# Modulation panels of the opening stretch multiplied in two portions, with projection chunks between them

## The chip, the cores and the metric

The kernel runs on one core of a Trainium2 chip. Its time is the device time of one execution in microseconds (us), lower is better. The kernel before took 673.79 us, the median of three executions (672.49 to 673.83).

## The reference

One inference step of a hybrid diffusion backbone with one layer: 128 context tokens and 512 latent tokens of 1024 features, all in float32. The parts that the edited stretch computes are the first lines:

```python
mod = silu(cond) @ w_mod + b_mod      # (2, 6*1024): one row per condition (latent, context)
shift1, scale1, gate1, shift2, scale2, gate2 = split(mod, 6)
h = rmsnorm(x, g_pre1) * (1 + scale1) + shift1
z = h @ w_in                          # columns [q | k | v | B | C | u], 512 each
```

After them come differential attention in four heads, a gated short convolution in 512 channels, the output projection, and a hierarchical mixture of 16 experts. They are not touched.

## The kernel before

There is one program for each engine, written out in order, and semaphores between them. An engine executes its program strictly in that order, so the order of the TensorE program around the change is the order written in the source.

**Modulation panels.** Before any column of h exists, shift1 and scale1 are needed, 2048 columns of `w_mod`. They are computed in four panels. Panel n brings 256 columns of shift and the same 256 of scale, that is what the feature chunks 2n and 2n+1 of h need (a chunk is 128 of the 1024 features). `mod_early(n)` multiplies the conditions (32 columns wide, two of them used) by the panel: 8 matmuls, k = 0 to 7, over the 8 chunks of the contraction. Matmul k writes the strip of 32 partitions that begins at 32 * (k % 4) in bank 4 + n % 2 of PSUM, so each strip collects two of them. The panel's weights come in four loads r = 0 to 3, load r with k = 2r and 2r+1, in a ring of eight slots; each pair of matmuls signals `mod_q`.

**From a panel to h.** VectorE adds the bias (`mod_rows_out`, L1207), TensorE turns the rows to columns and sums strips by four transposes (`mod_cols`, L1727) with a reduction on VectorE (L1213 in `mod_columns`), which then writes the shift B1 and factor A1 of two chunks and signals `a1_ready`. For each chunk k, TensorE transposes four latent blocks of x (`h_transposes(k)`, L1763; the context block in `ctx_transposes`, L1756, four chunks at a time), ScalarE applies A1 and B1 to the 512 latent columns (L797), VectorE to the 128 context columns (`h_ctx`, L1229), ScalarE rounds all 640 (L801), and VectorE forms the rest that the rounding left (`h_lo`, L1234, signals `hT_ctx`). Products use three passes over such rounded and rest parts. The weights of the projection are split in the same way, ScalarE (L782) and VectorE (`split_lo`, L1200).

**Projection chunks.** `z_first(k)` (L1772) multiplies chunk k for three token blocks at once: banks 3, 6 and 7, three passes each, 9 matmuls. It waits for `hT_ctx` of its chunk, and for the weights' split at even k. The eight chunks are set between the panels by hand. After chunk 7 the row products `z_rows` (L1839) follow, 24 matmuls a block, with modulation groups and transposes between them.

**Queues.** SyncE issues all weight loads in order: panel n's eight DMAs (L462), then load n of the projection's first weights (L489). From panel 2 on a load waits until the slot's old load is multiplied. GpSimd waits for the fourth `a1_ready` ahead of the loads of the rope tables (L621 to L623).

`lam_mm` are two products with one column each for the scalar lambda. They write columns of banks 6 and 3, which chunk 0 writes later; VectorE copies them out first (`lam_cp`).

Of the kernel before, what the change touches and what calls it, by code (L numbers as in the profile page):

```python
# [29 lines left out]
P = 128  # L30
D = 1024
KC = D // P
# [4 lines left out]
H, DV, DQ = 4, 128, 64  # L37
# [9 lines left out]
MOD_EARLY = 4  # L47
# [16 lines left out]
def build(nc, a):  # L64
# [16 lines left out]
    with ctx:  # L81
        def sb(name, shape, dt=F32):
            return ctx.enter_context(nc.sbuf_tensor(name, shape, dt))
# [20 lines left out]
        ones = sb("ones", [P, P])  # L104
# [7 lines left out]
        ps = ctx.enter_context(nc.psum_tensor("ps", [P, 8, N], F32))  # L112
# [14 lines left out]
        def col(i, n=1):  # L127
            return small[:, i:i + n]
# [7 lines left out]
        lamp = col(99)  # L136
        nlam = col(100)
        epsc = col(101)
        lamw = col(102, 4)
# [81 lines left out]
        def early_slot(j):  # L221
            return qkv[:, (j % 8) * D:(j % 8 + 1) * D]
# [945 lines left out]
        def _(dve):  # L1168
            n_chain = [0]

            def link(ins):
                n_chain[0] += 1
                ins.then_inc(S["dve_chain"], 1)
                dve.wait_ge(S["dve_chain"], n_chain[0])
# [10 lines left out]
            link(nc.vector.tensor_copy(small[:, 16:39], ps[:, 6, 0:23]))  # L1185
            link(ts(subg, subg, 1.0 - LAM_INIT, None, ALU.mult))
            tt(lamp, lamq[:, 0:1], lamq[:, 1:2], ALU.mult).then_inc(S["lam_prod"], 1)

            dve.wait_ge(S["rms1"], 1)
            link(nc.vector.reciprocal(rstd, rt))  # L1190
# [3 lines left out]
            def split_lo(item):  # L1194
                kind, c, r = item
                n = place[kind, c]
                m = 6 * P if kind == "conv" else QUARTER
                slot, rslot = (4 * n + r) % SPLIT, at_ring[item] % RAW
                dve.wait_ge(S["hi"], 4 * n + r + 1)
                tt(spl[:, slot, 1, 0:m], raw[:, rslot, 0:m], spl[:, slot, 0, 0:m].bitcast(F32), ALU.subtract).then_inc(S["lo"], 1)  # L1200

            def mod_rows_out(n):
                dve.wait_ge(S["mod_q"], 4 * (n + 1))
                if n >= 2:
                    dve.wait_ge(S["col_mm"], n - 1)
                both = lambda ap, m: ap.rearrange("p (s n) -> p s n", s=2)[:, :, m:m + CHUNK]
                tt(both(rows_early[n % 2], 0), both(ps[:, 4 + n % 2, :], 0), both(bias_early, n * CHUNK), ALU.add).then_inc(S["mod_ev"], 1)  # L1207

            def mod_columns(n):
                dve.wait_ge(S["col_mm"], n + 1)  # L1210
                ks = slice(2 * n, 2 * n + 2)
                parts = ps[:, 4 + n % 2, :].rearrange("p (j g m) -> p j m g", j=4, g=4)[:, :, 0:2, :]
                link(nc.vector.reduce_sum(cols_early.rearrange("p (j c) -> p j c", c=2), parts, axis=AX))  # L1213
                sh = cols_early[:, 0:4].rearrange("p (k c) -> p c k", c=2)
                sc = cols_early[:, 4:8].rearrange("p (k c) -> p c k", c=2)
                nc.vector.tensor_copy(B1[:, :, ks], sh)
                stt(A1[:, 0, ks], sc[:, 0, :], 1.0, gpre1[:, ks], ALU.add, ALU.mult)
                link(stt(A1[:, 1, ks], sc[:, 1, :], 1.0, gpre1[:, ks], ALU.add, ALU.mult))
                ts(col(183), epsc, 1.0, None, ALU.mult).then_inc(S["a1_ready"], 1)

            def hf_rows(k):
                return work[:, TOK * (k % 2):TOK * (k % 2 + 1)]

            def h_ctx(k):
                dve.wait_ge(S["h_trc"], k // 4 + 1)
                if k >= 2:
                    dve.wait_ge(S["hT_ctx"], k - 1)
                o = (k % 4) * P
                ts(hf_rows(k)[:, L_LAT:TOK], ps[:, 2, o:o + P], A1[:, 1, k:k + 1], B1[:, 1, k:k + 1],  # L1229
                   ALU.mult, ALU.add).then_inc(S["hf_ctx"], 1)  # L1230

            def h_lo(k):
                dve.wait_ge(S["hT_lat"], k + 1)
                tt(hS[:, 1, k, :], hf_rows(k), hS[:, 0, k, :].bitcast(F32), ALU.subtract).then_inc(S["hT_ctx"], 1)  # L1234
            dve.wait_ge(S["bmod_in"], 16)
            mod_rows_out(0)
            split_lo(("in", 0, 0))
            mod_columns(0)
            h_ctx(0)
            h_ctx(1)  # L1240
            h_lo(0)
            dve.wait_ge(S["lam_mm"], 1)
            nc.vector.tensor_copy(lamw[:, 0:1], ps[:, 6, 0:1]).then_inc(S["lam_cp"], 1)
            nc.vector.tensor_copy(lamw[:, 1:2], ps[:, 3, 0:1]).then_inc(S["lam_cp"], 1)
            for n in range(1, MOD_EARLY):
                mod_rows_out(n)
                h_lo(2 * n - 1)
                split_lo(("in", 0, n))
                mod_columns(n)
                h_ctx(2 * n)  # L1250
                h_lo(2 * n)
                h_ctx(2 * n + 1)
            h_lo(KC - 1)
            split_lo(SPLITS[2][0])

            def rope_rows(g):
# [446 lines left out]
        def _(pe):  # L1703
            mm = nc.tensor.matmul
# [3 lines left out]
                    pe.wait_ge(S["lo"], 4 * n + k // 2 + 1)  # L1708
            PASSES = ((0, 0), (0, 1), (1, 0))

            def mod_early(n):
                if n >= 2:
                    pe.wait_ge(S["a1_ready"], n - 1)
                for k in range(KC):
                    j = 4 * n + k // 2
                    if k % 2 == 0:
                        pe.wait_ge(early[j % 8], 32 * (j // 8 + 1))
                    g = 32 * (k % 4)
                    ins = mm(ps[g:g + 32, 4 + n % 2, :], condz[:, k, :], early_slot(j)[:, (k % 2) * N:(k % 2 + 1) * N],
                             start=(k < 4), stop=(k >= 4))  # L1720
                    if k % 2:
                        ins.then_inc(S["mod_q"], 1)

            def mod_cols(n):
                pe.wait_ge(S["mod_ev"], n + 1)
                for j in range(4):
                    ins = nc.tensor.transpose(ps[:, 4 + n % 2, j * P:(j + 1) * P], rows_early[n % 2][:, j * P:(j + 1) * P], ident[:, :])  # L1727
                ins.then_inc(S["col_mm"], 1)
# [20 lines left out]
            def ctx_transposes(f):  # L1749
                if f == 0:  # L1750
                    pe.wait_ge(S["xn_ready"], TB)
                else:
                    pe.wait_ge(S["hf_ctx"], 4)
                for j in range(4):
                    k = 4 * f + j
                    ins = nc.tensor.transpose(ps[:, 2, j * P:(j + 1) * P], x[:, CTX, k * P:(k + 1) * P], ident[:, :])  # L1756
                ins.then_inc(S["h_trc"], 1)

            def h_transposes(k):
                if k >= 2:  # L1760
                    pe.wait_ge(S["hf_lat"], k - 1)
                for b in range(4):
                    ins = nc.tensor.transpose(ps[:, k % 2, b * P:(b + 1) * P], x[:, b, k * P:(k + 1) * P], ident[:, :])  # L1763
                ins.then_inc(S["h_tr"], 1)

            def z_first(k):
                n = place["in", 0]
                pe.wait_ge(S["hT_ctx"], k + 1)
                part_ready(n, k)
                for g, bank in enumerate((3, 6, 7)):  # L1770
                    for s, m in PASSES:
                        ins = mm(ps[:, bank, :], hS[:, s, k, g * P:(g + 1) * P], weight(n, k, m),  # L1772
                                 start=(k == 0 and s + m == 0), stop=(k == KC - 1 and s == 1))
                    if k == KC - 1:
                        ins.then_inc(S["z_mm"], 1)
# [4 lines left out]
            pe.wait_ge(S["stage_in"], 16 * 7)  # L1780
            nc.tensor.transpose(ps[:, 6, 0:23], vrow, ident[0:23, 0:23]).then_inc(S["rows_tr"], 1)
            pe.wait_ge(S["cols_ready"], 2)
            mod_early(0)
            ctx_transposes(0)
            h_transposes(0)
            h_transposes(1)
            mod_cols(0)
            pe.wait_ge(S["lam_prod"], 1)
            mm(ps[:, 6, 0:1], ones[0:DQ, :], lamp[0:DQ, :], start=True, stop=True)
            mm(ps[:, 3, 0:1], ones[DQ:P, :], lamp[DQ:P, :], start=True, stop=True).then_inc(S["lam_mm"], 1)  # L1790
            mod_early(1)
            pe.wait_ge(S["lam_cp"], 2)
            z_first(0)
            mod_cols(1)
            h_transposes(2)
            h_transposes(3)
            z_first(1)
            mod_early(2)
            z_first(2)
            mod_cols(2)  # L1800
            ctx_transposes(1)
            h_transposes(4)
            h_transposes(5)
            z_first(3)
            mod_early(3)
            z_first(4)
            mod_cols(3)
            h_transposes(6)
            h_transposes(7)
            z_first(5)  # L1810
            z_first(6)
            z_first(7)

# [450 lines left out]
```

## Time and profile before

| | us |
|---|---|
| median of three executions | 673.79 |
| the profiled execution, its own time | 672.04 |
| its span, first to last instruction | 670.1 |
| TensorE (PE) busy | 639.0, 95% |
| VectorE (DVE) busy | 510.9, 76% |
| ScalarE (ACT) busy | 416.0, 62% |
| GpSimd (POOL) busy | 110.8, 17% |
| matmuls and weight loads | 3570 each |

The mean granted clock of TensorE is 0.995 of full speed. "PE" is a matmul, "PEld" the load of its stationary operand beside it; queues that issue DMAs have a q behind the engine's name (SPq is SyncE's). The ends of matmuls are modelled, so that one printed duration holds a fixed latency that the next matmul overlaps; what a group occupies is read from its start to the start of the next group. The 8 float32 matmuls of a panel are recorded as 16 instructions.

### The profile page before, as it was taken

The numbers are of one execution on the slowest core, as the hardware profiler recorded it, in microseconds if no ns is written. First come the engines' busy times: TensorE is split into PE (matmuls) and PEld (weight loads), VectorE is DVE, ScalarE is ACT, GpSimd is POOL, SyncE is SP. The second block draws the span as 40 slices with busy tenths as digits, with TensorE's granted clock in tenths as the row PEclk, the third lists the DMA queues.
The fourth block names the chain that finished last, engine by engine and source line by source line (L and its number), as shares of the span: only waits on it lengthen the run. The fifth ranks groups of instructions, "written<-read, shape, count | busy, mean of one in ns | idle before, by whom it ended". The sixth has DMA issues, their size and how long they took to land.

```text
span 670.1 us, 11052 instructions
## 1 busy us (share of the span) xinstructions
PE 639.0 (95%) x3570; PEld 524.3 (78%) x3570; DVE 510.9 (76%) x755; ACT 416.0 (62%) x640; POOL 110.8 (17%) x172
## 2 busy tenths in 40 slices
PE   2999999999999999999998899999999999999993
PEld 0577767889999998888786688888888888888872
DVE  2666576767676767775876988898989999899986
ACT  5552122344747486763445687888888888888873
POOL 2041000165000000000011650000000000290151
PEclk9999999999999999999999999999999999999997
DMA  9965768549212134495488799999999999999886
GB/s 332 386 244 184 264 242 254 156 148 336 64 34 59 62 101 151 147 324 189 159 313 320 251 336 419 419 420 420 420 420 420 420 420 419 416 403 376 320 308 157
DMA packets 77148, 188.16 MB, mean 281 GB/s; under 512 B 7824, under 2 KB 29381, under 8 KB 77109
## 3 DMA queue, kind: packets, MB, share of 16 engines
q1 hardware_dynamic: 65408, 153.11, 61.9%
q0 software_dynamic: 7392, 22.47, 9.8%
q10 hardware_dynamic: 4310, 12.10, 4.5%
q8 instruction: 22, 0.36, 0.2%
q14 instruction: 16, 0.12, 0.0%
HBM read 166.12 MB, written 21.53 MB: 280 GB/s over the span
## 4 chain that ended last, share of the span: by engine, by line
PE 77%; DVE 6%; DMA 6%; POOL 3%; ACT 2%; SPq 2%; issue 2%; POOLq 0%; ACTq 0%; DVEq 0%
PE ps L2128 20%; PE ps L2148 11%; PE ps L1839 10%; PE ps L1863 7%; PE ps L1895 6%; PE ps L1867 5%; PE ps L1916 3%; PE ps L1939 2%; PE ps L1772 2%; PE ps L2104 2%; SPq L462 2%; DMA catT_mem<-token_rows,rows_now 2%; PE ps L1930 2%; PE ps L1737 1%; DMA expert_rows<-catT_mem 1%
## 5 line engine op out<-in xcount | busy, mean ns | idle before, releaser
L2128 PE MATMUL ps<-split_ring,split_rows 128*128 128x512 f32 x720 | 168.3, 392 | 1.7 <-DVE split_rows L1568 1.0
L1485 DVE TENSOR_TENSOR split_ring<-qkv_mem,split_ring 128x1024 fp32r<-128x1024 f32 x124 | 144.0, 1221 | 23.4 <-ACT split_ring L970 23.2
L2128 PEld LDWEIGHTS ps<-split_ring,split_rows 128*128 128x128 f32 x720 | 133.9, 188 | 30.3 <-DVE split_ring L1485 1.6
L970 ACT CAST split_ring<-qkv_mem 128x1024 fp32r<-128x1024 f32 x124 | 121.1, 1053 | 9.3 <-ACT catT_mem L1076 9.3
L1863 PE MATMUL ps<-split_rows,split_ring 128*128 128x384 f32 x288 | 87.1, 349 | 0.2 <-ACT work L905 0.2
L2148 PE MATMUL ps<-split_ring,split_rows 128*128 128x512 f32 x360 | 86.3, 395 | 0.0
L2148 PEld LDWEIGHTS ps<-split_ring,split_rows 128*128 128x128 f32 x360 | 66.6, 188 | 13.6
L1867 PE MATMUL ps<-split_rows,split_ring 128*128 128x256 f32 x288 | 77.0, 280 | 0.0
L1485 DVE TENSOR_TENSOR split_ring<-raw_ring,split_ring 128x1024 fp32r<-128x1024 f32 x64 | 74.3, 1221 | 0.0
L1839 PE MATMUL ps<-split_ring,split_rows 128*128 128x512 f32 x288 | 68.0, 393 | 0.0
L970 ACT CAST split_ring<-raw_ring 128x1024 fp32r<-128x1024 f32 x64 | 62.4, 1046 | 0.9 <-DMA raw_ring<-in_w_exp_up 0.9
L1839 PEld LDWEIGHTS ps<-split_ring,split_rows 128*128 128x128 f32 x288 | 53.4, 188 | 10.8
L782 ACT CAST split_ring<-raw_ring 128x1024 fp32r<-128x1024 f32 (+1 forms) x36 | 34.2, 959 | 41.2 <-DMA raw_ring<-in_w_in 41.2
L1895 PE MATMUL ps<-split_ring,split_rows 128*128 128x512 f32 x240 | 58.4, 396 | 0.7 <-DVE split_ring L1200 0.7
L1200 DVE TENSOR_TENSOR split_ring<-raw_ring,split_ring 128x1024 fp32r<-128x1024 f32 (+1 forms) x36 | 39.5, 1102 | 23.3 <-ACT split_ring L782 22.9
L1863 PEld LDWEIGHTS ps<-split_rows,split_ring 128*128 128x128 f32 x288 | 53.5, 189 | 1.4 <-issue 1.3
L1867 PEld LDWEIGHTS ps<-split_rows,split_ring 128*128 128x128 f32 x288 | 53.4, 188 | 0.0
L1895 PEld LDWEIGHTS ps<-split_ring,split_rows 128*128 128x128 f32 x240 | 44.0, 188 | 10.3 <-DVE split_ring L1200 1.0
L1341 DVE TENSOR_REDUCE small<-ps 128x1 f32<-128x640 f32 (+1 forms) x40 | 26.8, 712 | 12.9 <-PE ps L1916 12.7
L1064 ACT CAST split_rows<-ps 128x512 fp32r<-128x512 f32 x30 | 16.1, 590 | 32.3 <-PE ps L2104 32.3
L626 POOL DMA_DIRECT2D x_rows<-in_b_mod x10 | 5.1, 513 | 181.5 <-DMA out_lat<-x_rows 181.5
L674 POOL TENSOR_TENSOR rows_now<-token_lists 128x1 uint32<-128x1 uint32 x13 | 5.2, 396 | 169.3 <-PE ps L2104 169.2
(361 smaller groups left out, 919.1 us busy)
## 6 DMA issues: line engine op xcount, KB each, us to landing
qkv_mem<-in_w_exp_gate SPq DMA_DIRECT2D x64, 512.0 KB, 8.3
qkv_mem<-in_w_exp_up SPq DMA_DIRECT2D x60, 512.0 KB, 7.0
raw_ring<-in_w_exp_down SPq DMA_DIRECT2D x60, 512.0 KB, 8.0
raw_ring<-in_w_mod SPq DMA_DIRECT2D x26, 512.0 KB, 4.5
qkv_mem<-in_w_mod SPq DMA_DIRECT2D x32, 256.0 KB, 7.0
expert_rows<-catT_mem ACTq DMA_DIRECT2D x14, 512.0 KB, 6.6
expert_rows<-work POOLq DMA_DIRECT2D x26, 256.0 KB, 5.9
raw_ring<-in_w_in SPq DMA_DIRECT2D x12, 512.0 KB, 6.4
```

The source lines that it names most:

```text
L782: nc.scalar.copy(spl[:, (4 * n + r) % SPLIT, 0, 0:m], raw[:, q % RAW, 0:m]).then_inc(S["hi"], 1)
L970: nc.scalar.copy(moe_split(tile, j, r, 0), moe_raw(tile, j, r)).then_inc(S["hi"], 1)
L1200: tt(spl[:, slot, 1, 0:m], raw[:, rslot, 0:m], spl[:, slot, 0, 0:m].bitcast(F32), ALU.subtract).then_inc(S["lo"], 1)
L1341: nc.vector.reduce_max(nm[:, u % 2, c:c + 1], psf[:, SC[c]:SC[c] + nk], axis=AX, negate=True).then_inc(S["neg_max"], 1)
L1485: tt(moe_split(tile, j, r, 1), moe_raw(tile, j, r), moe_split(tile, j, r, 0).bitcast(F32), ALU.subtract).then_inc(S["lo"], 1)
L1839: ins = mm(ps[:, g % 2, :], hS[:, s, k, b * P:(b + 1) * P], weight(n, k, m), start=(k == 0 and s + m == 0), stop=(k == KC - 1 and s == 1))
L1863: return mm(ps[:, CONV_BANK, 0:LOW], conv_weight(n, k, s, part), hS[:, m, k, 0:LOW], start=(k == 0 and s + m == 0), stop=(k == KC - 1 and ...
L1867: return mm(ps[:, CONV_BANK + 1, 0:HIGH], conv_weight(n, k, s, part), hS[:, m, k, LOW:TOK], start=(k == 0 and s + m == 0), stop=(k == KC - ...
L1895: ins = mm(ps[:, banks + j, :], cS[:, s, b, kk, :], weight(place["o", j], kk, m), start=(kk == 0 and s + m == 0), stop=(kk == KC - 1 and s ...
L1916: ins = mm(psf[:, SC[c] + o:SC[c] + o + m], q[rows, :], key[rows, :], start=(s + w == 0), stop=(s == 1))
L2128: ins = mm(ps[:, j, :], rows[:, s, k * P:(k + 1) * P], moe_split(tile, j, k // 2, m)[:, (k % 2) * N:(k % 2 + 1) * N], start=(k == 0 and s ...
L2148: ins = mm(ps[:, 5 + half, :], aS[:, s, k, :], spl[:, moe_split_slot(turn, j, k), m, half * N:(half + 1) * N], start=(k == 0 and s + m == ...
```

## The change

TensorE multiplies loads 0 to 2 of panels 1, 2 and 3, then a projection chunk, and then load 3 of the panel. Two of the three banks of the next odd chunk come ahead of the panel's column transposes, its third bank behind them. The column transposes of panel 0 go ahead of the transposes of chunk 1. Chunk 5 goes ahead of the transposes of chunks 6 and 7, chunk 3 ahead of those of 4 and 5. The lambda products go to the front of the program. VectorE's program becomes one loop over panels, with `split_lo` behind `mod_columns` and `h_ctx`, and the lambda copies ahead of the norm's reciprocal.

```diff
@@ VectorE, start
             tt(lamp, lamq[:, 0:1], lamq[:, 1:2], ALU.mult).then_inc(S["lam_prod"], 1)
+            dve.wait_ge(S["lam_mm"], 1)
+            nc.vector.tensor_copy(lamw[:, 0:1], ps[:, 6, 0:1]).then_inc(S["lam_cp"], 1)
+            nc.vector.tensor_copy(lamw[:, 1:2], ps[:, 3, 0:1]).then_inc(S["lam_cp"], 1)
@@ VectorE, panels
-            mod_rows_out(0)
-            split_lo(("in", 0, 0))
-            mod_columns(0)
-            h_ctx(0)
-            h_ctx(1)
-            h_lo(0)
-            dve.wait_ge(S["lam_mm"], 1)
-            nc.vector.tensor_copy(lamw[:, 0:1], ps[:, 6, 0:1]).then_inc(S["lam_cp"], 1)
-            nc.vector.tensor_copy(lamw[:, 1:2], ps[:, 3, 0:1]).then_inc(S["lam_cp"], 1)
-            for n in range(1, MOD_EARLY):
+            for n in range(MOD_EARLY):
                 mod_rows_out(n)
-                h_lo(2 * n - 1)
-                split_lo(("in", 0, n))
                 mod_columns(n)
                 h_ctx(2 * n)
+                split_lo(("in", 0, n))
                 h_lo(2 * n)
                 h_ctx(2 * n + 1)
-            h_lo(KC - 1)
+                h_lo(2 * n + 1)
             split_lo(SPLITS[2][0])
@@ TensorE, helpers
-            def mod_early(n):
+            def mod_early(n, rs=range(4)):
...
-                for k in range(KC):
+                for k in (2 * r + i for r in rs for i in range(2)):
...
-            def z_first(k):
+            def z_first(k, gs=range(3)):
...
-                for g, bank in enumerate((3, 6, 7)):
+                for g in gs:
+                    bank = (3, 6, 7)[g]
@@ TensorE, order
             pe.wait_ge(S["cols_ready"], 2)
+            pe.wait_ge(S["lam_prod"], 1)
+            mm(ps[:, 6, 0:1], ones[0:DQ, :], lamp[0:DQ, :], start=True, stop=True)
+            mm(ps[:, 3, 0:1], ones[DQ:P, :], lamp[DQ:P, :], start=True, stop=True).then_inc(S["lam_mm"], 1)
             mod_early(0)
             ctx_transposes(0)
             h_transposes(0)
+            mod_cols(0)
             h_transposes(1)
-            mod_cols(0)
-            pe.wait_ge(S["lam_prod"], 1)
-            mm(ps[:, 6, 0:1], ones[0:DQ, :], lamp[0:DQ, :], start=True, stop=True)
-            mm(ps[:, 3, 0:1], ones[DQ:P, :], lamp[DQ:P, :], start=True, stop=True).then_inc(S["lam_mm"], 1)
-            mod_early(1)
+            mod_early(1, range(3))
             pe.wait_ge(S["lam_cp"], 2)
             z_first(0)
+            mod_early(1, (3,))
+            h_transposes(2)
+            z_first(1, (0, 1))
             mod_cols(1)
-            h_transposes(2)
+            z_first(1, (2,))
             h_transposes(3)
-            z_first(1)
-            mod_early(2)
+            mod_early(2, range(3))
             z_first(2)
+            mod_early(2, (3,))
+            z_first(3, (0, 1))
             mod_cols(2)
+            z_first(3, (2,))
             ctx_transposes(1)
             h_transposes(4)
             h_transposes(5)
-            z_first(3)
-            mod_early(3)
+            mod_early(3, range(3))
             z_first(4)
+            mod_early(3, (3,))
+            z_first(5, (0, 1))
             mod_cols(3)
+            z_first(5, (2,))
             h_transposes(6)
             h_transposes(7)
-            z_first(5)
             z_first(6)
             z_first(7)
```

## Rows read from the trace of the kernel before

**Rows 1.** The page: busy time of the engines, and the chain that ended last.
```profile
PE 639.0 (95%) x3570; PEld 524.3 (78%) x3570; DVE 510.9 (76%) x755; ACT 416.0 (62%) x640; POOL 110.8 (17%) x172
PE 77%; DVE 6%; DMA 6%; POOL 3%; ACT 2%; SPq 2%; issue 2%; POOLq 0%; ACTq 0%; DVEq 0%
```
**Rows 2.** Waits of TensorE: line, waited for, us in total, times, longest.
```profile
PE ps L1719 <- DMA qkv_mem<-in_w_mod: 3.5, 3, 2.9
...
PE ps L2104 <- DMA catT_mem<-token_rows,token_lists: 2.2, 1, 2.2
```
**Rows 3.** Busy time in stretches: stretch, its us, engines, PEclk, DMA share, GB/s.
```profile
360.00:375.00 15.00, 11.79 (x56) 9.17 (x55) 11.89 (x30) 7.72 (x10) 2.73 (x4) 1.00 0.74 262
...
400.00:600.00 200.00, 199.56 (x947) 166.15 (x946) 181.28 (x180) 162.31 (x191) 32.92 (x44) 1.00 1.03 419
```
**Rows 4.** Timeline of TensorE, 12 to 56 us: start, us, instructions, idle before.
```profile
12.36 5.84 PE L1719 MATMUL ps<-qkv_mem,cond_columns 128*32 128x512 f32 x16 [2.90 <-DMA qkv_mem<-in_w_mod]
...
20.34 1.07 PE L1719 MATMUL ps<-qkv_mem,cond_columns 128*32 128x512 f32 x8
21.74 1.05 PE L1719 MATMUL ps<-qkv_mem,cond_columns 128*32 128x512 f32 x4 [0.34 <-DMA qkv_mem<-in_w_mod]
23.09 1.05 PE L1719 MATMUL ps<-qkv_mem,cond_columns 128*32 128x512 f32 x4 [0.30 <-DMA qkv_mem<-in_w_mod]
24.07 2.34 PE L1772 MATMUL ps<-split_ring,split_rows 128*128 128x512 f32 x9
...
29.75 1.92 PE L1719 MATMUL ps<-qkv_mem,cond_columns 128*32 128x512 f32 x16
...
33.79 0.60 PE L1727 MATMUL ps<-ident,catT_mem 128*128 128x128 f32 x4
...
34.66 1.04 PE L1763 MATMUL ps<-ident,x_rows 128*128 128x128 f32 x8
...
41.76 0.60 PE L1727 MATMUL ps<-ident,catT_mem 128*128 128x128 f32 x4
...
42.99 2.33 PE L1772 MATMUL ps<-split_ring,split_rows 128*128 128x512 f32 x9
45.60 4.44 PE L1772 MATMUL ps<-split_ring,split_rows 128*128 128x512 f32 x18 [0.28 <-DVE split_rows L1234]
49.87 5.60 PE L1839 MATMUL ps<-split_ring,split_rows 128*128 128x512 f32 x24
55.40 1.06 PE L1737 MATMUL ps<-raw_ring,cond_columns 128*32 128x512 f32 x8
```
**Rows 5.** Timeline of TensorE, 29.7 to 30.5 us: the first half of panel 2.
```profile
29.75 1.06 PE L1719 MATMUL ps<-qkv_mem,cond_columns 128*32 128x512 f32 x8
```
**Rows 6.** Timeline of VectorE, 18 to 46 us.
```profile
18.31 0.69 DVE L1207 TENSOR_TENSOR catT_mem<-ps,catT_mem 128x512 f32<-128x512 f32 x1 [1.06 <-PE ps L1719]
...
41.05 1.22 DVE L1200 TENSOR_TENSOR split_ring<-raw_ring,split_ring 128x1024 fp32r<-128x1024 f32 x1
42.40 0.19 DVE L1213 TENSOR_REDUCE small<-ps 128x8 f32<-128x32 f32 x1
...
43.05 0.41 DVE L1229 TENSOR_SCALAR work<-ps,small 128x128 f32<-128x128 f32 x1
44.72 0.82 DVE L1234 TENSOR_TENSOR split_rows<-work,split_rows 128x640 fp32r<-128x640 f32 x1 [1.26 <-ACT split_rows L801]
```
**Rows 7.** Timeline of ScalarE, 35 to 45 us.
```profile
35.34 0.78 ACT L797 ACTIVATE work<-ps,small 128x512 f32<-128x512 f32 x1 [3.16 <-PE ps L1763]
...
43.15 0.78 ACT L797 ACTIVATE work<-ps,small 128x512 f32<-128x512 f32 x1 [3.33 <-DVE small L1219]
43.96 0.73 ACT L801 CAST split_rows<-work 128x640 fp32r<-128x640 f32 x1
```
**Rows 8.** Timelines of SyncE and GpSimd, 24 to 46 us: DMA issues.
```profile
24.67 5.84 SPq L462 DMA_DIRECT2D qkv_mem<-in_w_mod  x8
...
42.30 7.00 SPq L489 DMA_DIRECT2D raw_ring<-in_w_in  x2
...
43.42 1.76 POOL L621 DMA_DIRECT2D catT_mem<-rope  x2 [38.51 <-DVE small L1219]
```

## The prediction

> **What bounds the kernel now.** I read the page first, then the waits of TensorE, then its busy time in stretches, and last the timelines of the first 55 us, because the whole diff lies there.
>
> The page shows a TensorE that is busy 95% of the span and holds 77% of the chain that ended last [rows 1]. Its waits name what is left: the start of the kernel, and single waits of 1 to 2 us around 365 to 385 us [rows 2]. In the expert stage it is busy 199.6 of 200 us, with the DMA engines full beside it [rows 3]. So a microsecond that TensorE loses early has nowhere to be made up, and only idle time that it has today can be won.
>
> How much is that in the edited stretch? In the timeline of TensorE [rows 4] look for the bracket with an idle time. Between the first panel (12.36) and 49.87, where the row products of L1839 begin, there are three: 0.34 and 0.30 ahead of panel 1's third and fourth loads, and 0.28 ahead of chunk 6 at 45.60. Everything else is back to back. The edit's prize is thus about 1 us; what matters is what it costs.
>
> **Prices.** From the starts in [rows 4], since the printed ends overlap:
> - A projection chunk is 9 matmuls (3 banks, 3 passes). 24 of the same shape go from 49.87 to 55.40, 0.230 each: 2.07 a chunk, 1.38 for two banks, 0.69 for one.
> - Eight transposes go from 33.79 to 34.66: 0.435 for four.
> - A whole modulation panel, with its entry and exit: 33.79 to 41.76 is 7.97. In it are 16 transposes (1.74), two chunks (4.14) and one panel, which is left with 2.09.
> - A panel in portions. A panel is 8 matmuls, recorded as 16 instructions, that write four strips of 32 partitions (k mod 4). Load r brings k = 2r and 2r+1, so loads 0 and 1 fill four strips, load 2 strips 0 and 1, load 3 strips 2 and 3. The first 8 instructions of an undisturbed panel take 1.06 [rows 5]. The 4 of a single load take 1.05, both at 21.74 and at 23.09, and loads 0 and 1 together took 1.07 at 20.34 [rows 4]. So four instructions on two strips last as long as eight on four: strips run side by side, and half of them save nothing. Hence a portion of three loads costs what all four cost (2.09), and load 3 by itself costs a panel less two of its four time slots: 2.09 less (1.92 less 1.05) = 1.22. Its bounds: 0.44, a quarter of 1.92 less its tail, if the slot were shared after all, and 1.37, which is 1.05 with an entry and exit of 0.16 each. I take 1.22.
>
> **The change, part by part.**
>
> 1. The two lambda products and their two copies go ahead of panel 0. TensorE waits for the first load until 12.36 and VectorE for rms1 long after; behind the products loads 2 and 3 of panel 1 are waited for anyway. Worth 0 (bounds: 0.3 won, 0.3 lost).
>
> 2. Panel 0's column transposes go ahead of chunk 1's transposes. They need mod_rows_out(0), VectorE at 18.31 plus 0.69 = 19.00 [rows 6], when eight transposes have just ended, so they start at about 19.05. From here a chain returns that I use four times. Read it after panel 3: column transposes at 41.76 [rows 4]; VectorE reduces at 42.40 (+0.64) and has A1 and B1 written by 43.1; ScalarE's ACTIVATE starts at 43.15 (0.75 after the reduce), its CAST at 43.96 [rows 7]; h_lo at 44.72 [rows 6]; TensorE's chunk at 45.60. From reduce to chunk 3.20, from ACTIVATE to chunk 2.45. In the new VectorE order h_ctx (0.41) and split_lo (1.22) stand between reduce and h_lo; they end 2.2 after the reduce, h_lo could start at 2.32 at the earliest, so they are hidden behind ScalarE. For chunk 0: 19.05 + 0.64 + 3.20 = 22.9. TensorE has by then done loads 0 to 2 of panel 1 (21.74 + 1.05 = 22.8). Chunk 0 starts at 22.9 instead of 24.07: 1.17 won.
>
> 3. Then the order is walked with the prices; a restart after a wait costs 0.1 as in 45.60 (the 18 there take 4.27, not 4.14). Chunk 0 ends 25.07, load 3 26.29, transposes 2 26.73, two banks of chunk 1 28.11, columns 1 28.55, third bank 29.24, transposes 3 29.68, three loads of panel 2 31.77. Chunk 2 may start at 28.11 + 0.64 + 3.20 = 31.95: wait 0.2. Then it ends 34.12, load 3 35.34, two banks 36.72, columns 2 37.16, third bank 37.85, context transposes 38.29, transposes 4 and 5 39.16, three loads of panel 3 41.25. Chunk 4 hangs on ScalarE's ACTIVATE, which starts about 0.25 after transposes 4 (34.66 + 0.44 to 35.34 before [rows 4, 7]): 38.72 + 0.25 + 2.45 = 41.42: wait 0.2. It ends 43.59, load 3 44.81, two banks 46.19, columns 3 46.63, third bank 47.32, transposes 6 and 7 48.19.
>
> 4. Now chunk 6. Before, chunk 5's nine matmuls lay between transposes 7 and chunk 6 and covered the chain but for 0.28. In the new order chunk 5 is used up ahead of the transposes. ACTIVATE 6 waits for A1 (46.19 + 0.64 + 0.75 = 47.58) and for transposes 6 (47.76 + 0.25 = 48.01); chunk 6 starts at 48.01 + 2.45 = 50.46. TensorE has nothing from 48.19 on: a wait of 2.3 in place of the 0.28. Chunk 7's rows are ready 1.9 after that, in time.
>
> So chunk 6 starts at 50.46 against 45.60: **4.9 us later**. The same by causes: start -1.2; load 3 by itself, three times 1.22, +3.65; two waits of 0.2, each with a restart, +0.6; the longer wait for chunk 6, +1.8 (its restart was there before, and so were 0.45: the recorded 0.28 is counted from a modelled end, chunk 5 had been issued by 42.99 + 0.08 + 2.07 = 45.15); together +4.9. I take 4.8.
>
> What else moves: the DMA issues. SyncE's loads of panel 3 begin at 24.67 and end at 30.5 [rows 8]; the last waits for load 3 of panel 1, now at 26.3 instead of 24.1, while its issue comes near 29: nothing. The ring's next load waits for the fourth split, 42.3 before (41.05 + 1.22, [rows 6, 8]), about 49 now; it feeds the second part of the projection, two blocks of row products (11 us) behind chunk 7. GpSimd's rope loads wait for the last A1, 43.4 before [rows 8], about 47.7 now, less late than TensorE. All later waits shift with TensorE. The cost passes through whole; I see no slack that would hide more than 0.5 of it.
>
> The clock: the granted clock is 1.00, its 2.4 GHz level, from 360 to 375 us [rows 3], and in that stretch TensorE stood idle for 2.2 us before L2104 [rows 2]. My new wait is 2.3, so I leave the clock alone. The Trainium skill, TensorE: Matmul & The Clock Gate, section HAM oscillation, warns that waits between bursts of matmuls can drop the clock to half, and that this cost is paid anew at each burst. By that rule the 18 matmuls of chunks 6 and 7 would take 8.3 instead of 4.1 and the sum be about 9.
>
> **Against what time.** The profiled execution took 672.04 (span 670.1, 1.9 around it); the three others 672.49, 673.79 and 673.83. The middle of the four is 673.1. With 4.8 the likely median is 677.9.
>
> **Rivals.**
> - *The single load is cheap* (0.44 to 0.5 instead of 1.22, three times): 2.2 less, +2.6, 675.7. For it: [rows 4] show single loads only right after a DMA wait. Against: 20.34 and 29.75 are not after one and have the same slots. 11%.
> - *The clock falls* in the wait for chunk 6: +9, 682. Against: the idle time of 2.2 at clock 1.00. 4%.
> - *Not slower*: the expert stage is set by its weight stream, not by TensorE (DMA share 1.03 in [rows 3]), and the stream starts at a time that the early stretch doesn't move. Place: 400 to 600 us; price: the whole 4.8 back; it decides if TensorE there has 4.8 us of waiting for weights hidden in its modelled ends. Then 673. Against: it issues without a wait in that stretch, and SyncE's first expert loads stand behind waits for TensorE's results. 4%.
> - *The new waits don't appear*, since the split gives ScalarE and VectorE their rows earlier: then the single loads and the earlier start remain, +2.4, 675.5. For it: chunks 0 to 5 do get their rows earlier. Against: the chain to chunk 6 begins at the column transposes of panel 3, and just 0.69 + 0.87 of work stands behind them. 6%.
>
> **How the numbers follow.** The forecast has 75%. This kernel tells no change from one of about 0.2% (1.3 us). Slower by more: the forecast and three rivals, 0.95 with a little for their neighbours, less what I may have misread as a whole: 0.93. Within: 0.04. Faster: 0.03. The range runs from the cheap loads, 675.7 less 0.7 for a low set of executions, to +6 on an execution of 673.8 with a bit of the bounds of load 3: 675.0 to 680.6.
>
> **What would show it.** Right: load 3 as groups of four instructions of 1.05 beside chunks; L1772 starting near 22.9; a wait of about 2.3 on h_lo (L1234 before) ahead of the last 18 matmuls; the first x24 of the row products near 54.7. Wrong: that start under 53, or a wait for chunk 6 under 1.5, or the tail of the kernel not shifted by what the early stretch lost.

## The result and the profile after

The changed kernel takes 677.83 us in the median of eight executions (675.88 to 679.54); the kernel before, with eight of its own, 673.66 (672.00 to 676.18). The ratio is 1.0067, with an interval from 1.0047 to 1.0087: slower, by 4.5 us (3.2 to 5.9) by the ratio and by 4.2 between the medians. Forecast were 677.9 and +4.8. A second set of ten, taken beside the experiments, gave 677.55 and 1.0060 (1.0033 to 1.0086). The profiled execution took 677.10 with a span of 675.1, against 672.04 and 670.1.

The timeline of TensorE after, to be read against [rows 4] (L1712 is the panel, L1720 the column transposes, L1749 and L1756 the transposes of x, L1766 the chunks; start, us, instructions, idle before):

```profile
20.00 1.45 PE L1712 MATMUL ps<-qkv_mem,cond_columns 128*32 128x512 f32 x8
21.72 1.05 PE L1712 MATMUL ps<-qkv_mem,cond_columns 128*32 128x512 f32 x4 [0.27 <-DMA qkv_mem<-in_w_mod]
22.92 2.33 PE L1766 MATMUL ps<-split_ring,split_rows 128*128 128x512 f32 x9
25.17 1.05 PE L1712 MATMUL ps<-qkv_mem,cond_columns 128*32 128x512 f32 x4
...
29.70 1.91 PE L1712 MATMUL ps<-qkv_mem,cond_columns 128*32 128x512 f32 x12
31.88 2.33 PE L1766 MATMUL ps<-split_ring,split_rows 128*128 128x512 f32 x9 [0.27 <-DVE split_rows L1237]
34.14 1.05 PE L1712 MATMUL ps<-qkv_mem,cond_columns 128*32 128x512 f32 x4
35.12 1.66 PE L1766 MATMUL ps<-split_ring,split_rows 128*128 128x512 f32 x6
36.62 0.60 PE L1720 MATMUL ps<-ident,catT_mem 128*128 128x128 f32 x4
...
41.32 2.31 PE L1766 MATMUL ps<-split_ring,split_rows 128*128 128x512 f32 x9 [0.26 <-DVE split_rows L1237]
...
46.03 0.60 PE L1720 MATMUL ps<-ident,catT_mem 128*128 128x128 f32 x4
46.38 0.94 PE L1766 MATMUL ps<-split_ring,split_rows 128*128 128x512 f32 x3
47.16 1.04 PE L1756 MATMUL ps<-ident,x_rows 128*128 128x128 f32 x8
50.29 4.43 PE L1766 MATMUL ps<-split_ring,split_rows 128*128 128x512 f32 x18 [2.10 <-DVE split_rows L1237]
54.56 5.60 PE L1839 MATMUL ps<-split_ring,split_rows 128*128 128x512 f32 x24
```

Three things are to be seen. Twelve instructions of a panel take 1.91, as sixteen did (1.92, [rows 4]), and the last four take another 1.05. The wait ahead of chunk 6 is 2.10 instead of 0.28. And the row products start at 54.56 instead of 49.87: 4.69 of the span's 5.0 are lost by this point.

The chain that makes chunk 6 wait, on VectorE and on ScalarE (against [rows 6, 7]):

```profile
46.67 0.19 DVE L1216 TENSOR_REDUCE small<-ps 128x8 f32<-128x32 f32 x1 [1.32 <-PE ps L1720]
...
47.73 0.41 DVE L1232 TENSOR_SCALAR work<-ps,small 128x128 f32<-128x128 f32 x1 [0.34 <-issue]
48.06 1.22 DVE L1203 TENSOR_TENSOR split_ring<-raw_ring,split_ring 128x1024 fp32r<-128x1024 f32 x1
49.41 0.83 DVE L1237 TENSOR_TENSOR split_rows<-work,split_rows 128x640 fp32r<-128x640 f32 x1
```
```profile
47.85 0.78 ACT L797 ACTIVATE work<-ps,small 128x512 f32<-128x512 f32 x1 [4.49 <-DVE small L1222]
48.66 0.72 ACT L801 CAST split_rows<-work 128x640 fp32r<-128x640 f32 x1
```

From ScalarE's ACTIVATE to chunk 6 it is 2.44, as before (43.15 to 45.60). The chain has not become longer; TensorE has nothing left to do during it.

Behind the row products the shift stays. The waits of TensorE there, after (against [rows 2]):

```profile
PE ps L2104 <- DMA catT_mem<-token_rows,token_lists: 2.3, 1, 2.3
PE ps L2104 <- DMA catT_mem<-token_rows,rows_now: 1.0, 1, 1.0
```

The same transposes L2104 start at 371.56 instead of 366.80 (+4.76), and at 408.03 instead of 402.72 (+5.31, a gather of token rows came 0.5 later in this execution); the end is 5.0 later.

### The profile page after: what moved, and what is told of

The parts are those of the page before. It is cut to its first block, busy times and chain, and to the rows that moved or that the text cites. A ratio compares the mean times of both kernels' runs of the same rounds, so it can differ in the third digit from the quotient of the medians.

```text
span 675.1 us, 11054 instructions
## 1 busy us (share of the span) xinstructions
PE 644.4 (95%) x3570; PEld 526.8 (78%) x3570; DVE 511.3 (76%) x755; ACT 416.2 (62%) x640; POOL 111.6 (17%) x172
## 4 chain that ended last, share of the span: by engine, by line
PE 76%; DVE 6%; DMA 6%; POOL 3%; ACT 3%; issue 2%; SPq 2%; POOLq 0%; ACTq 0%; DVEq 0%
PE ps L2128 20%; PE ps L2148 11%; PE ps L1839 10%; PE ps L1863 7%; PE ps L1895 6%; PE ps L1867 5%; PE ps L1916 3%; PE ps L1939 2%; PE ps L1766 2%; PE ps L2104 2%; DMA catT_mem<-token_rows,rows_now 2%; PE ps L1930 2%; SPq L462 2%; PE ps L1730 1%; DMA catT_mem<-token_rows,token_lists 1%
```

## The experiments

Where a trace gives the verdict I compare starts on TensorE up to the row products. They repeat within 0.1 once it is allowed for that the landing of panel 1's loads moves by up to 0.8 from execution to execution; the whole times of one kernel scatter by 2.4 to 7.1 us. Each ratio is against executions of the kernel before that were taken beside it.

**Whole panels in the new order.**

```diff
-            mod_early(1, range(3))
+            mod_early(1)
...
             z_first(0)
-            mod_early(1, (3,))
```
(panels 2 and 3 likewise)

> The changed kernel with panels 1 to 3 multiplied whole again; the new order of transposes, chunks and of VectorE stays. My theory (a single load by itself costs a half-filled panel, about 1.2 us, and chunk 6 waits because chunk 5 lies ahead of the transposes): chunk 0 starts at 24.1, the three portions of 1.2 are gone, the wait ahead of chunk 6 stays near 2; chunk 6 starts near 48.0 and the row products (L1839) at 52.2, that is 2.3 later than before and 2.3 earlier than the changed kernel; whole time 2.3 us over before. Rival (single loads are cheap, the order alone is the loss): row products at 54 or later. Rival (the portions are the whole loss): row products at 50 to 50.5.

```profile
22.98 1.05 PE L1712 MATMUL ps<-qkv_mem,cond_columns 128*32 128x512 f32 x4 [0.27 <-DMA qkv_mem<-in_w_mod]
...
31.82 3.73 PE L1766 MATMUL ps<-split_ring,split_rows 128*128 128x512 f32 x15 [0.25 <-DVE split_rows L1237]
...
40.08 3.76 PE L1766 MATMUL ps<-split_ring,split_rows 128*128 128x512 f32 x15 [0.24 <-DVE split_rows L1237]
...
47.94 4.38 PE L1766 MATMUL ps<-split_ring,split_rows 128*128 128x512 f32 x18 [2.10 <-DVE split_rows L1237]
52.16 5.60 PE L1836 MATMUL ps<-split_ring,split_rows 128*128 128x512 f32 x24
```

Chunk 6 at 47.94 and row products at 52.16, to a tenth where my theory had them. So at the row products the new order, VectorE's with it, costs 2.3 (52.16 less 49.87) and the portions 2.4 on top (54.56 less 52.16). Both rivals, each with one cause for everything, fall.

The whole times do not show this division. They are 676.05 us (10 executions), ratio 1.0058 (1.0039 to 1.0076): 3.9 us over before, 2.6 to 5.1, and the 2.3 that I expected lies outside. The profiled execution is the fastest of the ten (673.95) and its span is only 1.9 longer than before. Against the changed kernel's 1.0067 and 1.0060 the ratio is barely lower, though 2.4 us would be 0.0036, and each has an uncertainty of about 0.002. What the other executions lost behind the stretch no trace shows.

**Two and two loads.**

```diff
-            mod_early(1, range(3))
+            mod_early(1, (0, 1))
...
             z_first(0)
-            mod_early(1, (3,))
+            mod_early(1, (2, 3))
```
(panels 2 and 3 likewise)

> The changed kernel with each panel in loads 0 and 1, the chunk, then loads 2 and 3. My theory (four strips run side by side, so a portion of two loads with all four strips costs the same 1.2 as a single load with two strips): the second portions are x8 lasting 1.05 to 1.10 as the x4 did, the first portions shorter by a half-filled slot pair (0.9), which the waits ahead of chunks 2 and 4 take up (0.27 becomes about 1.1); row products at 54.5, no change of the time against the changed kernel. Rival (cost goes by the number of instructions): each second portion 0.5 to 1.0 longer, row products 1.5 or more later, at 56.

```profile
29.71 1.06 PE L1712 MATMUL ps<-qkv_mem,cond_columns 128*32 128x512 f32 x8
31.89 2.36 PE L1766 MATMUL ps<-split_ring,split_rows 128*128 128x512 f32 x9 [1.11 <-DVE split_rows L1237]
34.18 1.06 PE L1712 MATMUL ps<-qkv_mem,cond_columns 128*32 128x512 f32 x8
35.17 1.67 PE L1766 MATMUL ps<-split_ring,split_rows 128*128 128x512 f32 x6
...
50.45 6.01 PE L1766 MATMUL ps<-split_ring,split_rows 128*128 128x512 f32 x18 [2.10 <-DVE split_rows L1237]
56.29 5.61 PE L1839 MATMUL ps<-split_ring,split_rows 128*128 128x512 f32 x24
```

Eight instructions on four strips take 1.06 where four on two took 1.05, and what the first portion saves (1.91 less 1.06) goes into the wait ahead of chunk 2 (1.11 instead of 0.27). Up to chunk 6 this kernel runs as the changed one (50.45 against 50.29). So the number of instructions does not set the cost, the fullest strip does. But the row products start at 56.29, the place that I had given to the rival. The second portions are not longer, though, as the rival needs; the cause is another. TensorE in stretches of this run (stretch, its us, busy, PEclk, DMA share, GB/s):

```profile
50.40:52.00 1.60, 1.55 (x7) 0.97 0.83 223
52.00:55.40 3.40, 3.40 (x10) 0.51 0.83 258
```

The granted clock fell to its lower level, 1.2 GHz, at 51.9 and came back at 55.3. TensorE had then been busy again for 1.4 us behind its wait of 2.10 ahead of chunk 6. Chunks 6 and 7 took 1.6 longer (6.01 against 4.43). The time was 677.48 (6 executions), ratio 1.0075 (1.0051 to 1.0099), not to be told from the changed kernel's.

**Chunk 5 back behind the transposes.**

```diff
             mod_early(3, (3,))
-            z_first(5, (0, 1))
             mod_cols(3)
-            z_first(5, (2,))
             h_transposes(6)
             h_transposes(7)
+            z_first(5)
             z_first(6)
```

> The changed kernel with chunk 5 as a whole behind the transposes of chunks 6 and 7, as before; the portions stay. My theory: panel 3 now ends behind chunk 4, so its column transposes have to wait for VectorE's bias rows (end near 45.35, a wait of about 0.8), then 3.84 to chunk 6, with 3.4 of work over it: chunk 6 at 49.25 after a wait of 0.4 to 0.5, row products at 53.5, 1.0 earlier than the changed kernel. Rival (the place of chunk 5 is the whole cause of the wait ahead of chunk 6): row products at 52.5 or earlier. Rival (chunk 6 hangs on something else, the split of the weights or GpSimd): no change, 54.5.

```profile
43.23 1.05 PE L1712 MATMUL ps<-qkv_mem,cond_columns 128*32 128x512 f32 x4
45.08 0.66 PE L1720 MATMUL ps<-ident,catT_mem 128*128 128x128 f32 x4 [0.79 <-DVE catT_mem L1210]
...
49.16 4.42 PE L1766 MATMUL ps<-split_ring,split_rows 128*128 128x512 f32 x18 [0.46 <-DVE split_rows L1237]
53.41 5.60 PE L1838 MATMUL ps<-split_ring,split_rows 128*128 128x512 f32 x24
```

As expected: the wait ahead of chunk 6 shrinks from 2.10 to 0.46, and a new one of 0.79 opens ahead of the column transposes, because the panel's last load now ends right before them and they need VectorE's bias rows. From load 3 of panel 3 to the row products it is 10.18, against 11.00 in the changed kernel (43.56 to 54.56): 0.8 won, of 1.0 expected. So the place of chunk 5 makes the long wait ahead of chunk 6; about half of the 1.6 taken off it comes back as the other wait, which in the changed kernel two banks of chunk 5 had covered. The 0.46 that is left is VectorE's order, as the next kernels show. The whole time does not show the 0.8: 676.71 (6 executions), ratio 1.0068 (1.0042 to 1.0094), the changed kernel's.

**Only the first panel in portions**, everything from chunk 1 on in the old order. The edit of the TensorE order is shown against the kernel before; the lambda products, panel 0's column transposes and VectorE's program are as in the changed kernel.

```diff
-            mod_early(1)
+            mod_early(1, range(3))
             pe.wait_ge(S["lam_cp"], 2)
             z_first(0)
-            mod_cols(1)
+            mod_early(1, (3,))
             h_transposes(2)
             h_transposes(3)
+            mod_cols(1)
             z_first(1)
```

> The kernel before with the early part of the change alone: lambda products first, column transposes of panel 0 ahead of chunk 1's transposes, panel 1 in portions with chunk 0 between, VectorE's new order; all behind as before. My theory: chunk 0 starts at 22.9, 1.15 earlier, but load 3 behind it costs 1.2, so chunk 2 starts at 31.6 as before and the row products at 49.8 to 49.9; same time as before. Rival (filling the wait for the load wins 1 us): row products at 48.8. Rival (VectorE's new order costs, its split now in the chain): row products at 50.5 or later.

```profile
22.93 2.33 PE L1766 MATMUL ps<-split_ring,split_rows 128*128 128x512 f32 x9 [0.29 <-issue]
25.18 1.05 PE L1712 MATMUL ps<-qkv_mem,cond_columns 128*32 128x512 f32 x4
...
31.55 2.37 PE L1766 MATMUL ps<-split_ring,split_rows 128*128 128x512 f32 x9
...
45.76 4.45 PE L1766 MATMUL ps<-split_ring,split_rows 128*128 128x512 f32 x18 [0.47 <-DVE split_rows L1237]
50.05 5.61 PE L1834 MATMUL ps<-split_ring,split_rows 128*128 128x512 f32 x24
```

672.69 against 672.79, ratio 1.0001 (0.9986 to 1.0016). Chunk 0 starts 1.14 earlier and chunk 2 as before (31.55 against 31.60). Even where the multiplication of a load was waited for, starting the chunk first gives nothing: the load's 1.2 comes after it. Chunk 6 is 0.16 late, which I hadn't counted.

**VectorE's new order without portions**: the kernel above with panel 1 whole and its column transposes ahead of the transposes of chunks 2 and 3. The lambda products and panel 0's column transposes stay at their new places.

```diff
-            mod_early(1, range(3))
+            mod_early(1)
             pe.wait_ge(S["lam_cp"], 2)
             z_first(0)
-            mod_early(1, (3,))
+            mod_cols(1)
             h_transposes(2)
             h_transposes(3)
-            mod_cols(1)
```

> The kernel before with the lambda products first, the column transposes of panel 0 ahead of chunk 1's transposes, and VectorE's new order; panels whole, chunks in the old order. My theory: chunk 0 starts at 24.0 as before (load 3 lands at 23.05), and the one cost is VectorE's: with the panel in portions alone chunk 6 had started 0.15 late, because the split of the weights now stands between h_ctx and h_lo of chunk 6 and h_ctx starts 0.4 late; row products at 50.0, against 49.87. Time the same as before within 0.2%. Rival (that 0.15 came from the portions): row products at 49.8.

```profile
22.30 1.05 PE L1712 MATMUL ps<-qkv_mem,cond_columns 128*32 128x512 f32 x4 [0.28 <-DMA qkv_mem<-in_w_mod]
...
45.00 4.45 PE L1766 MATMUL ps<-split_ring,split_rows 128*128 128x512 f32 x18 [0.47 <-DVE split_rows L1237]
49.29 5.61 PE L1833 MATMUL ps<-split_ring,split_rows 128*128 128x512 f32 x24
```

Load 3 landed 0.79 earlier here (22.30 against 23.09); from it to the row products it is 26.99 against 26.78 before, so 0.2 is lost behind load 3. The wait ahead of chunk 6 is 0.47, as with the portions: the 0.16 did not come from them. VectorE's timeline has the cause: h_ctx starts at 42.66, 0.34 after the engine was free, and the split of the weights behind it holds h_lo until 44.12, while ScalarE's CAST had ended at 43.90. 673.66, ratio 1.0000 (0.9976 to 1.0025).

**Filling the gaps.** Where TensorE waits for loads 2 and 3 of panel 1, transposes fit that have to be done anyway; and the bank split of the change, used on chunk 4, covers VectorE's step ahead of panel 3's column transposes, with chunk 5 left behind them. Panels 2 and 3 stay whole; VectorE's new order stays. The edit is shown against the kernel just above.

```diff
             h_transposes(1)
-            mod_early(1)
+            mod_early(1, (0, 1))
             pe.wait_ge(S["lam_cp"], 2)
+            h_transposes(2)
+            mod_early(1, (2,))
+            h_transposes(3)
+            mod_early(1, (3,))
             z_first(0)
             mod_cols(1)
-            h_transposes(2)
-            h_transposes(3)
...
             mod_early(3)
-            z_first(4)
+            z_first(4, (0, 1))
             mod_cols(3)
+            z_first(4, (2,))
```

> A version meant to beat both: the panels 2 and 3 whole, panel 1's loads 2 and 3 with the transposes of chunks 2 and 3 in the waits ahead of them, two banks of chunk 4 ahead of panel 3's column transposes. My theory: the transposes (0.87) go into gaps of 0.3 and 0.3 plus the gap ahead of load 1, so chunk 0 starts at 24.3 with them done; chunk 6 starts at 44.6 (wait near 0.2), row products at 48.9 to 49.0, 0.9 earlier than before; whole time about 0.9 less (0.13%). Rival (each entry and exit of a portion costs what the gaps give): row products at 49.5 or later.

```profile
23.47 1.05 PE L1712 MATMUL ps<-qkv_mem,cond_columns 128*32 128x512 f32 x4
24.45 2.34 PE L1766 MATMUL ps<-split_ring,split_rows 128*128 128x512 f32 x9
...
42.49 6.80 PE L1766 MATMUL ps<-split_ring,split_rows 128*128 128x512 f32 x27
49.12 5.60 PE L1836 MATMUL ps<-split_ring,split_rows 128*128 128x512 f32 x24
```

Chunk 0 starts at 24.45 (24.3 expected), the row products at 49.12, 0.75 earlier than before. Counted from the end of loads 0 and 1 of panel 1 it is 27.73 (from 21.39) against 28.46 (from 21.41 before), 0.73 less. The filling was not free: load 3 starts at 23.47 instead of 23.09, so 0.4 is paid there for 0.87 of transposes. 671.81 (12 executions), ratio 0.9978 (0.9955 to 1.0000). The second version also sets the transposes of chunk 6 ahead of panel 3, and one bank of chunk 4 ahead of the column transposes, two behind:

```diff
             z_first(3)
+            h_transposes(6)
             mod_early(3)
-            z_first(4, (0, 1))
+            z_first(4, (0,))
             mod_cols(3)
-            z_first(4, (2,))
-            h_transposes(6)
+            z_first(4, (1, 2))
             h_transposes(7)
```

> As the kernel before it in this list, but the transposes of chunk 6 stand ahead of panel 3 and only one bank of chunk 4 ahead of its column transposes, so that the chain to chunk 6 begins 0.25 earlier and does not wait for transposes. My theory: no wait left ahead of chunk 6, which starts at 44.4; row products at 48.7, whole time 1.2 less than before (0.17%). Rival (VectorE, not the transposes, sets chunk 6, by h_ctx and the weights' split): chunk 6 at 44.6 or later, row products at 48.9.

```profile
38.72 0.96 PE L1766 MATMUL ps<-split_ring,split_rows 128*128 128x512 f32 x3
39.62 0.66 PE L1720 MATMUL ps<-ident,catT_mem 128*128 128x128 f32 x4
...
41.87 6.43 PE L1766 MATMUL ps<-split_ring,split_rows 128*128 128x512 f32 x27
48.13 5.60 PE L1836 MATMUL ps<-split_ring,split_rows 128*128 128x512 f32 x24
```

Its row products came at 48.13 with loads that landed 0.8 earlier (its loads 0 and 1 ended at 20.61, those of the first version at 21.39); from there 27.52 against 27.73, so 0.2 better. With the first version's landing that is 48.9, the number of the rival and not my 48.7, yet not by the rival's cause. Small idle times are not printed here, so read the starts: 27 matmuls of 0.230 are 6.21, and chunks 5 to 7 take 6.26 (41.87 to 48.13) where the first version took 6.63. The wait ahead of chunk 6 is gone, as I expected. What I missed is 0.2 ahead of the column transposes (0.90 from the start of one bank, 0.69, to theirs): VectorE's bias rows end at 39.57. 671.40 (12 executions), ratio 0.9982 (0.9955 to 1.0009). Both once more:

> The first of the two versions that fill the gaps, once more to narrow its interval: by its trace the row products come 0.75 earlier than before once the landing of panel 1's loads is the same. My theory: whole time 0.8 under before, ratio 0.9988; with both sets an interval that lies below 1. Rival (the single executions scatter by more and the first set's 0.9978 was luck, the gain gets lost later): ratio at or above 1.

672.41, ratio 0.9996 (0.9972 to 1.0019). The profile repeats the early stretch, 27.71 instead of 27.73. An interval below 1 is not reached.

> The second version that fills the gaps, once more: its trace shows 0.2 less than the first between the end of loads 0 and 1 of panel 1 and the row products. My theory: ratio 0.9985, not told from the first version by times. Rival (no gain that reaches the end): ratio at or above 1.

671.87, ratio 0.9987 (0.9967 to 1.0007), and 27.52 again in the early stretch. All four ratios lie below 1 and all four intervals reach it: the traces show 0.73 and 0.94 won in the early stretch, the times don't prove that they reach the end.

**The changed kernel once more.**

> The changed kernel once more, beside the others on one chip. The early stretch repeats: row products at 54.4 to 54.6, wait of 2.1 ahead of chunk 6. The clock: in one kernel with the same wait ahead of chunk 6 it fell to half from 51.9 to 55.3 and the 18 matmuls of chunks 6 and 7 took 1.6 longer. If that is a matter of the execution and not of the kernel, this profile shows it or not, row products at 54.5 or at 56.1, and the executions spread by about that much.

```profile
50.20 4.41 PE L1766 MATMUL ps<-split_ring,split_rows 128*128 128x512 f32 x18 [2.10 <-DVE split_rows L1237]
54.45 5.60 PE L1839 MATMUL ps<-split_ring,split_rows 128*128 128x512 f32 x24
```

The early stretch repeats to a tenth, and the clock held through it: 677.55 (10 executions), ratio 1.0060 (1.0033 to 1.0086). So the wait of 2.10 by itself does not bring the fall; whole panels kept the full clock behind it too. Whether the fall seen with two and two loads belongs to that execution or to that kernel stays open. There is one profile of it, and that kernel has more idle time ahead, 1.1 before chunks 2 and 4 each. How often the changed kernel suffers such a fall two profiles can't say.

## Why the prediction was right

- *TensorE is the bound, an early loss passes through.* Right for the changed kernel: 4.69 at the row products, 4.76 at 371 us, 5.0 at the end, and 4.5 in the times. For whole panels the times gave 3.9 where the trace gave 2.3, so how much passes through is not shown there.
- *A single load costs a half-filled panel, 1.22.* Right in kind, shown by two and two loads (and at 34.14 and 43.56 without a DMA wait ahead, which the rows before could not show), and slightly too large: from chunk 2 at 31.88 to the column transposes at 36.62 are 4.74, less 15 matmuls (3.45) and a restart (0.1), 1.19; from 41.32 to 46.03 likewise 1.16.
- *Chunk 0 starts at 22.9.* It did (22.92); and the gain is no more than a loan, as the first panel alone showed. My sum had both entries, -1.2 and one of the three 1.22, without saying that they cancel.
- *Two waits of 0.2 at chunks 2 and 4.* 0.27 and 0.26; 31.88 and 41.32 against 31.95 and 41.42.
- *Chunk 6 waits 2.3 because chunk 5 is used up.* It started at 50.29, forecast 50.46. The wait and its cause were right: with chunk 5 put back it is 0.46, and 0.47 with whole panels in the old order but VectorE's new one. The price of 1.8 was not chunk 5's alone. Putting it back won 0.8, since its two banks had also covered VectorE's bias rows for panel 3, a wait of 0.79 that my sum did not look at because it never opened in this kernel.
- *The order of VectorE is hidden.* Nearly: where chunk 6 hardly waits it costs 0.16 (h_ctx starts 0.34 late, the split of the weights behind it then ends past ScalarE's CAST). In the changed kernel it is hidden, h_lo at 49.41 and the CAST's end at 49.38.
- *The DMA issues move nothing.* Right: the ring's next load was issued at 49.30 (about 49 forecast), the rope loads at 47.70, and TensorE is busy without a gap from 54.56 to 134.
- *The clock stays.* Right for both profiles of the changed kernel at that place, but by luck: my reason was one wait of 2.2 us at full clock. The fall happened after the same wait in a sister kernel, for 1.6 us and not the 4.1 that I had taken as its price, and after a wait of 2.3 late in this kernel's own first profile.

## What to carry to other kernels

A matmul that uses a part of the array's column strips is cheap only with neighbours in the other strips (here four instructions on two strips took 1.05 us, eight on four 1.06). So cut such a group so that each portion fills all strips, or don't cut it; here even that gained nothing, as the 0.85 saved went into a wait. Work that depends on nothing is the cover for the next chain: before a piece is moved ahead, look which wait it covers now. A gap behind a DMA is worth filling with work that must be done anyway and delays the waited piece by less than that work (0.4 for 0.87 here), not by swapping the waited piece behind other work.

## What the runs showed of the hardware

The clock fell at changing places. In the profile of the changed kernel it was at half from 372.8 to 379.6, beginning 1.2 us behind the wait of 2.3 ahead of L2104 (TensorE in stretches):

```profile
372.80:379.60 6.80, 6.03 (x17) 0.50 0.53 172
380.00:390.00 10.00, 9.94 (x54) 1.00 0.97 322
```

The kernel before kept its full clock behind the same wait, 2.2 [rows 2, 3]. The fall cost nothing there: from the transposes L2104 to the next ones it is 17.50 (371.56 to 389.06) against 17.49 (366.80 to 384.29), since the slower matmuls used up waits of 0.7 and 1.2 that follow in the kernel before. The later profiles of both gap-filling versions show a fall of 3.4 us from 383.1 and from 383.5, that of chunk 5 put back one from 388.4; the other profiles of this study show none while TensorE works. Each of these three began 1.6 to 2.1 us behind a wait of only 1.2 to 1.3, a wait that the profiles without a fall have as well.

What a fall costs depends on what follows. From the last of these transposes to the next ones (384.29 to 402.72 before) it is 18.0 at full clock, the wait for gathered rows (0.44 before) taken off, and 19.5 in all three profiles with the fall: 1.5 for 3.4 us at half clock. Between 51.9 and 55.3, where nothing waits, it was 1.6. One fall thus costs more than the gap filling wins (0.73 and 0.94). The changed kernel and both gap-filling versions have each one profile with a fall after 370 us and one without, so there it is not the kernel that decides; some of these profiles are of different chips. What starts a fall no run shows.

The Trainium skill, TensorE: Matmul & The Clock Gate, section Seeing it yourself, warns not to trust the single clock events of a trace fully, and to cross-check the total of throttled time against what it should cost. Here the matmuls agree with the events between 51.9 and 55.3, 18 of them in 6.01 instead of 4.43. The printed clock does not fit the matmuls in the first 18 us: it is 1.00 from 12 to 18 us in the kernel before, while an instruction of panel 0 lasted 1051 ns in the mean and one of panel 2 598 ns.
